# High-weight products of two blocks per unit at the head of a wide projection, and a later start of the modulation steps

## The reference, cut to what matters

```python
for l in range(DEPTH_2):
    mod = c_act @ w_ada[l] + b_ada[l]
    shift, scale, gate = jnp.split(mod, 3, axis=-1)
    h = _rmsnorm(x, norm_g[l]) * (1.0 + scale[:, None, :]) + shift[:, None, :]
    z = h @ w_in[l]                      # 2048 x 6656
    ...
    y = jnp.concatenate([o_fft, o_na, o_ret, o_cv], axis=-1) @ w_out[l]
    x = x + gate[:, None, :] * y
```

## Time and profile before

| | |
|---|---|
| median of the runs | 2070.2 us |
| the profiled execution | 2074.64 us |
| its span, first to last instruction | 2072.8 us |
| TensorE matmul, busy | 2032.5 us (98%) |
| TensorE weight load | 1642.6 us (79%) |
| VectorE | 1749.9 us (84%) |
| ScalarE | 1199.4 us (58%) |
| mean granted clock | 0.991 |
| mean transfer rate | 287 GB/s |

### The profile page before, as it was taken

How to read it: one execution, slowest core, us unless ns; L and a number is a source line. 1 busy time by engine, 2 the same in 40 slices (tenths; PEclk the granted TensorE clock), 3 DMA queues, 4 the chain that set the end, 5 groups by cost and what they waited for, 6 DMA issues and landing times.

```text
span 2072.8 us, 42606 instructions
## 1 busy us (share of the span) xinstructions
PE 2032.5 (98%) x18977; PEld 1642.6 (79%) x18977; DVE 1749.9 (84%) x1662; ACT 1199.4 (58%) x1079; POOL 58.3 (3%) x72
## 2 busy tenths in 40 slices
PE   8999999999999999999999999999999999999998
PEld 7889888888889946555555568888888888888887
DVE  7884798988888698999999989989967789899754
ACT  5553644444445488888877865465554444565543
POOL 0002300000000000000000000010000000100000
PEclk9999999999999999999999999999999999999999
DMA  7864487789898789999999977755857777558552
GB/s 282 323 221 145 163 316 284 275 315 328 321 329 300 282 310 405 420 420 420 420 420 418 411 274 263 258 192 201 291 199 287 271 290 255 196 203 293 181 203 102
DMA packets 96742, 595.27 MB, mean 287 GB/s; under 512 B 11176, under 2 KB 11336, under 8 KB 37808
## 3 DMA queue, kind: packets, MB, share of 16 engines
q1 hardware_dynamic: 94912, 583.66, 75.1%
q0 software_dynamic: 1648, 8.90, 1.1%
HBM read 588.32 MB, written 2.10 MB: 285 GB/s over the span
## 4 chain that ended last, share of the span: by engine, by line
PE 65%; issue 14%; DVE 11%; DMA 8%; ACT 2%; POOLq 0%; POOL 0%; DVEq 0%; ACTq 0%
PE GB L2274 43%; PE MB L2703 7%; PE GB L2703 6%; DVE w_lo L1321 3%; DMA W<-w_ada 3%; DMA Z<-w_ada 3%; DVE W L1321 2%; DMA raw<-w_down 2%; ACT w_hi L671 1%; DMA raw<-w_up 1%; DVE W L1292 1%; DVE Z L1292 1%; PE MB L2498 1%; PE MB L2474 1%; DVE Y L1382 1%
## 5 line engine op out<-in xcount | busy, mean ns | idle before, releaser
L1321 DVE SCALAR_TENSOR_TENSOR w_lo<-raw,w_hi 128x2048 f16<-128x2048 f32 x214 | 491.1, 2297 | 105.8 <-ACT w_hi L671 105.1
L671 ACT ACTIVATE w_hi<-raw 128x2048 f16<-128x2048 f32 x214 | 408.1, 1907 | 207.2 <-PE GB L2274 118.4
L2274 PE MATMUL GB<-H,w_hi 128*128 128x256 f16 x2880 | 476.0, 273 | 6.1 <-DVE w_lo L1321 4.3
L2274 PE MATMUL GB<-H,w_lo 128*128 128x256 f16 x1440 | 392.6, 273 | 0.0
L2274 PEld LDWEIGHTS GB<-H,w_hi 128*128 128x128 f16 x2880 | 279.5, 98 | 47.3 <-DVE w_lo L1321 6.4
L2274 PE MATMUL GB<-H,raw 128*128 128x256 f16 x2208 | 249.9, 273 | 8.3 <-DVE raw L1321 4.9
L2274 PEld LDWEIGHTS GB<-H,raw 128*128 128x128 f16 x2208 | 214.4, 98 | 40.1 <-DVE raw L1321 6.9
L1292 DVE SCALAR_TENSOR_TENSOR W<-W,SM 128x1024 f32<-128x1024 f32 x150 | 192.3, 1282 | 54.9 <-DMA W<-w_ada 51.4
L1321 DVE SCALAR_TENSOR_TENSOR raw<-raw 128x2048 f16<-128x2048 f32 x85 | 195.5, 2300 | 30.5 <-ACT raw L671 30.1
L671 ACT ACTIVATE raw<-raw 128x2048 f16<-128x2048 f32 x85 | 162.1, 1907 | 98.0 <-PE GB L2274 53.8
L2274 PEld LDWEIGHTS GB<-H,w_lo 128*128 128x128 f16 x1440 | 140.9, 98 | 16.4
(11 more groups left out here) (503 smaller groups left out, 3473.0 us busy)
## 6 DMA issues: line engine op xcount, KB each, us to landing
raw<-w_in SPq DMA_DIRECT2D x144, 1024.0 KB, 5.1
W<-w_ada SPq DMA_DIRECT2D x160, 512.0 KB, 5.8
raw<-w_out SPq DMA_DIRECT2D x48, 1024.0 KB, 5.9
raw<-w_down SPq DMA_DIRECT2D x35, 1024.0 KB, 13.3
raw<-w_up SPq DMA_DIRECT2D x29, 1024.0 KB, 12.5
raw<-w_gate SPq DMA_DIRECT2D x26, 1024.0 KB, 10.7
W<-w_down SPq DMA_DIRECT2D x17, 1024.0 KB, 13.1
raw<-xattn_wk SPq DMA_DIRECT2D x16, 1024.0 KB, 5.1
```

The costliest lines, as they stand in the source:

```text
L671: act.activation(w, raw_at[r], ACT.Copy, scale=W_SCALE).then_inc(hi_done, 1)
L1321: dve.scalar_tensor_tensor(lo, raw_at[r], W_SCALE, hi, ALU.mult, ALU.subtract).then_inc(raw_taken[r], 1)
L2274: last = pe.matmul(o, a, m, start=first, stop=end and w_part is lo, skip_group_check=True)
```

## The change

It has three parts. In `z0` and `z1` the first four blocks go through a new function `head` of TensorE: for each unit it takes the products with the high weights of two blocks (0 and 1, then 2 and 3), and after the last unit of the pair the products with their low weights, block by block, each block reported done after its low products. ScalarE makes the high splits of blocks 2 and 3 earlier, ahead of the units and after unit 6. The modulation steps of the two projections start with block 4 instead of block 2; of the 16, the three of blocks 2 and 3 are placed at 10, 11 and 13. `spread_root(3)` follows the four blocks.

```diff
     def halves(ph):
-        for m in [2, 2, 3, 4, 4, 5, 6, 6, 7, 8, 8, 9, 10, 12, 14, 16]:
+        for m in [4, 4, 5, 6, 6, 7, 8, 8, 9, 10, 10, 11, 12, 13, 14, 16]:
             put(ph, m)
...
             def shifted_hi(base, src, ph, shift):
+                split(ph, 2)
                 for n, unit in enumerate(UNITS):
                     act.wait_ge(S("norm_h"), base + n + 1)
...
                     if n == 6:
-                        split(ph, 2)
+                        split(ph, 3)
...
                 for m in range(4 * PIECES):
-                    if m >= 3:
+                    if m >= 4:
                         split(ph, m)
                     for i in nth(m, 3, 4, PIECES):
                         evict(i, 0)
...
+            def piece(ph, m, ks, parts, begins, ends):
+
+                s, (u, k) = where(ph, m)[1], (m % 2, m // 2)
+                ws = [a[slot(s)].rearrange("p (c n) -> p c n", c=8) for a in (hi_of, lo_of)]
+                for n in range(2):
+                    for c in ks:
+                        for x_low, w_low in parts:
+                            last = pe.matmul(GB[:, u, n * T:n * T + T], ws[w_low][:, c, n * P:n * P + P], (xh, xl)[x_low][:, 8 * k + c, :],
+                                             start=begins, stop=ends and c == ks[-1], skip_group_check=True)
+                            begins = False
+                return last
+
+            def head(ph, units, ready):
+
+                for k in range(2):
+                    for n, unit in enumerate(units):
+                        if unit[0] // 8 != k:
+                            continue
+                        first = unit[0] % 8 == 0
+                        pe.wait_ge(S("norm_lo"), ready + n + 1)
+                        for m in (2 * k, 2 * k + 1):
+                            s = where(ph, m)[1]
+                            if first:
+                                pe.wait_ge(hi_done, s + 1 + (s > at["z1"][1]))
+                                if k == 0:
+                                    pe.wait_ge(bank_free[m], uses[ph][m])
+                            piece(ph, m, [c % 8 for c in unit], ((0, 0), (1, 0)), first and k == 0, False)
+                    for m in (2 * k, 2 * k + 1):
+                        taken(pe, ph, m)
+                        piece(ph, m, range(8), ((0, 1),), False, k == 1).then_inc(block_done[where(ph, m)[1] % SPL], 1)
...
-                for m in range(4 * PIECES):
-                    if l == 0 and m == 3:
-                        spread_root(3, r_first)
+                head(ph, UNITS, 16 + 9 * l)
+                if l == 0:
+                    spread_root(3, r_first)
+                for m in range(4, 4 * PIECES):
```

## The result

The changed kernel took 2079.47 us (median of five, 2078.14 to 2085.42), the kernel before 2070.88 us beside it: a ratio of 1.0046, with a 95% interval of 1.0030 to 1.0061. The change makes the kernel slower by 8.6 us between the medians, 6 to 13 us by the interval; 2077.9 had been predicted, in a range of 2071.5 to 2082. The profiled execution was the slowest of the five, 2085.42 us with a span of 2083.5, so its sum has to be made against the 2074.6 of the profiled execution before: +10.8.

The account below looks back on a forecast made before the run. TensorE, busy for 98% of the span, was taken to bound the kernel. +4.2 us in `z0` and +3.5 in `z1` make +7.7 on the 2070.2 median: 2077.9 us, range 2071.5 to 2082.

Parts of the forecast that it names:

- Part 1, the head: First blocks of `z0` and `z1`: reordered products hide VectorE's chunk waits; -1.65 us up to block 3 in `z0`.
- Part 2, block 4: Unmoved eviction waits for block 2 and holds block 4: pauses 2.6 us (`z0`) and 3.2 (`z1`).
- rival (b): Block 4's splits are not held by the eviction, so the change is faster: -6.3 us, 2063.9; chance 0.06.
- Part 3, block 11: Modulation steps moved later delay VectorE's low split 11: block 11 +2.5 to +3.2 us (`z0`), +3.3 to +3.9 (`z1`).
- one more step is 1.2, or 1.9 with a wait of up to 0.7: VectorE between low splits 10 and 11: added modulation step costs 1.2 us, or 1.9 with a wait for its data.
- VectorE's idling between low splits 10 and 11 while TensorE pauses: Ahead of block 11: named as a sign that the prediction is wrong; no size given.
- The other queues: SP and GpSimd queues and `spread_root(3)` behind the head: zero, since final norms needing the spread stand behind low split 4.
- units 7 and 8: Chunk units late in the head: ready before TensorE asks, so nothing charged; the cover is 1.2 us.
- The clock: A half-clock stretch after block 4's pause costs 1.7 us of TensorE; counted zero, as block 11's pause swallows it.
- rival (c): Clock falls unswallowed, at block 11 or twice: +0.4 to +1.3 us per phase, up to 1.7 more; 2080.5; chance 0.14.
- The sum: Whole kernel: +4.2 us in `z0` and +3.5 in `z1`, together +7.7, giving 2077.9.

Follow-up runs that it names:

- changed, again: The changed kernel run once more with nothing edited (the sixth experiment), for a second profile: 2081.21 us, ratio 1.0040 to the kernel before.
- 1 evict behind: Changed kernel with ScalarE's eviction of piece 0, bank 0, put behind block 4's high split instead of ahead: 2069.68 us, ratio 0.9982.
- 2 steps back: Changed kernel with the modulation steps back at their old places, from block 2 on: 2075.36 us, ratio 1.0016.
- 3 steps only: Kernel before with only the modulation steps moved to block 4 on, its head unchanged: 2075.43 us, ratio 1.0008.
- 4 head only: 1 evict behind with the modulation steps at their old places: 2072.95 us, ratio 1.0001.
- 5 spread early: 1 evict behind with `spread_root(3)` also moved, ahead of block 2's low-weight products: 2066.26 us, ratio 0.9977.
- 7 no idle: Changed kernel with filler products of ones on TensorE, 22 (`z0`) or 28 (`z1`) ahead of block 4, 24 ahead of block 11: 2084.49 us, ratio 1.0061.
- 8 half the fillers: Changed kernel with 11 (`z0`) or 14 (`z1`) filler products ahead of block 4 and 11 ahead of block 11: 2080.00 us, ratio 1.0047.
- 9 first pair only: Changed kernel with only blocks 0 and 1 paired, blocks 2 and 3 in old order, three modulation steps at block 3: 2075.67 us, ratio 1.0021.
- 10 steps spread: 5 spread early with modulation steps starting at block 3, one instead of two at block 10, none at 11: 2068.55 us, ratio 0.9989.
- 11 small loads: Changed kernel with modulation loads of these stretches cut to a quarter of their bytes, read four times, steps unchanged: 2073.64 us, ratio 1.0012.

## Why the prediction was right

**Part 1, the head.** Forecast -1.65 us up to block 3 in `z0`. The table has the last group of blocks 3, 10 and 15, in us from the head's first product, read from TensorE's timelines.

```
kernel               z0: b3    b10    b15    z1: b3    b10    b15
before                24.10  61.39  88.63     23.70  61.19  87.69
changed               21.87  63.46  94.34     22.46  63.06  95.95
changed, again        21.87  61.79  91.79     21.87  63.19  91.72
1 evict behind        22.02  59.83  90.66     22.58  59.26  85.46
2 steps back          21.87  62.77  90.54     21.87  63.46  89.66
3 steps only          23.18  59.86  89.17     22.74  59.42  88.09
4 head only           21.87  63.06  90.83     22.60  61.35  88.48
5 spread early        22.30  58.98  88.58     21.87  58.55  85.16
7 no idle             21.87  63.89  95.45     21.87  64.80  96.36
8 half the fillers    21.87  61.79  91.40     21.87  61.79  90.44
9 first pair only     22.30  63.06  89.61     22.25  63.11  89.33
10 steps spread       22.30  62.02  89.02     21.87  59.02  85.22
11 small loads        21.87  63.26  89.55     22.57  62.49  88.68
```

Right: the head is 1.2 to 2.2 us shorter. In `z0` some 0.45 of that is the spread, which left block 3; with the spread counted in both kernels it is 1.8. The heads of 22.5 to 22.6 us in `z1` began with 3 us at 1.2 GHz (0.50 from 1658.50 to 1661.50 in the changed kernel); in the second execution that stretch was at 0.86, and the head took 21.87.

**Part 2, block 4.** The step that carried the prediction, and it held almost to the row. Forecast: eviction 20.35 us behind the head's start (1262.9 - 1242.55), measured 20.43 (1260.55 - 1240.12); low split 22.85, measured 22.86; block 4 25.15, measured 25.21; pauses 2.6 and 3.2, measured 2.63 + 0.16 and 3.07 + 0.16. The pause is decided by the order of two instructions in ScalarE's program: the one of experiment 1 took it away in both layers, the list of steps (experiment 2) and small loads (experiment 11) left it as it was. The whole loss hangs on it: the 1.0046 and 1.0040 become 0.9982 when the eviction alone is moved. What block 11 adds to it needs the late loads as well, since with small loads block 11 does not pause (experiment 11). With it fell rival (b): the split does not pass the eviction. The Trainium skill, "TensorE: Matmul & The Clock Gate", section "Architectural detail: the array is 16x 32x32, not 1x 128x128", says that ScalarE's and VectorE's queues are strictly first in, first out; the trace agrees: in this kernel and in those of experiments 2, 6 to 8 and 11 ScalarE idles 6.91 us, the eviction comes, and the split 0.49 to 0.50 us behind it.

**Part 3, block 11.** The mechanism was right, and the term for the load was too small. In the changed kernel low split 4 to 10 took 31.57 us in `z0` and 32.12 in `z1` (31.8 forecast). From 11 to 12 it took 1310.63 - 1304.35 = 6.28 and in `z1` 5.38; 6.29 and 5.38 had been forecast. What failed is 10 to 11: "one more step is 1.2, or 1.9 with a wait of up to 0.7", forecast 8.0 to 8.7 in `z0`, measured 9.80 (1304.35 - 1294.55) and 10.31 in `z1`. With small loads it is 8.20 (1294.26 to 1302.46), the working without the wait. So the step was sized nearly rightly (8.0 without a wait) and its load was not: 1.70 and 2.65 us of wait where 0.7 was the bound. The bound came from a wait at block 4, whose load had long been under way. The trace of before had longer ones in the same stretches, 1.16 us at 1294.72 in `z0`, and in `z1`:

```profile
1692.36 1.29 DVE L1292 SCALAR_TENSOR_TENSOR Z<-Z,SM 128x1024 f32<-128x1024 f32 x1 [2.38 <-DMA Z<-w_ada]
```

Low split 11 needs two steps, the second of which can load only when the step two before it has read its buffer; that chain should have been laid out. The prediction had named VectorE's idling between low splits 10 and 11 while TensorE pauses as a sign of being wrong. Half of it came: VectorE idled there, but 1.70 us that ended at 1300.51, while TensorE had products until 1303.57. Block 11 started 66.57 us behind the head in `z0` where it had been 62.53, +4.0 for a forecast of +2.5 to 3.2, and in `z1` 68.23 for 61.59, +6.6 for +3.3 to 3.9. In the second execution it was +1.5 and +3.6. For `z0` the forecast lies between the two executions, for `z1` at the lower one. That the total of 2077.9 came within 1.6 of the first median is for a part luck: the wait was put too small, and it varies by more than that from one execution to the next.

**The other queues.** Zero for `spread_root(3)` behind the head is right for the changed kernel and wrong as a price. VectorE had to wait for ScalarE until 1262.98 anyhow, and the spread was done at 1262.3. Experiment 1 took that cover off, and the spread cost VectorE 3.39 us. The prediction named no cover here, as it did for units 7 and 8.

**The clock.** Counted at zero, since the next pause, before block 11, was to swallow it. The clock fell behind block 4 of `z0`, and there it was swallowed as forecast: TensorE's last group of block 10 came at 63.46, 1.7 us later than at full clock, and VectorE let block 11 start only at 66.57. It also fell behind block 11, in both layers. Windows of the changed kernel from shortly behind block 4's start (the granted clock fell half a microsecond later) and from block 11 of `z0`, then from the same blocks of `z1`:

```profile
1265.87:1269.28 3.41, 3.41 (x18) 2.44 (x17) 3.31 (x4) 1.16 (x1) 0.00 (x0) 0.50 0.41 103
1306.69:1311.00 4.31, 4.31 (x25) 3.24 (x26) 4.27 (x9) 1.91 (x1) 0.00 (x0) 0.60 0.81 270
1684.30:1688.00 3.70, 3.70 (x34) 3.33 (x35) 3.59 (x3) 1.70 (x1) 0.00 (x0) 1.00 0.55 153
1726.66:1730.10 3.44, 3.38 (x16) 2.41 (x17) 3.44 (x8) 1.80 (x1) 0.00 (x0) 0.50 0.70 214
```

Nothing behind block 11 pauses long enough to give that back: blocks 11 to 15 took 27.7 to 27.8 us with such a stretch and 26.1 without one and without a pause (`z1` of experiment 1, both layers of experiment 9). That is rival (c)'s 1.7 us at block 11, in both layers of the first profile and one of the second. Where no late block 11 swallows it, the fall behind block 4 costs the same: from block 4's start to block 10's last group experiment 11 took 38.05 us in `z0`, with the fall, and 36.6 in `z1`, without, and experiment 9 took 38.25 in both layers, with it. Set against this, experiment 8 had no such stretch in its profile and no less time in its median, with the two reservations made there. So the step of counting the clock at zero holds at block 4 of `z0` alone; a fall costs 1.4 to 1.7 us where nothing swallows it, and how often one falls in the median execution stays open.

**The sum.** Forecast +4.2 and +3.5. The first profile has +5.7 and +8.3, nearly twice the forecast, the second (91.79 - 88.63, 91.72 - 87.69) +3.2 and +4.0, near it; the medians together +8.6 and +10.2. The mechanism at block 4 was right to a tenth of a microsecond; the load and the clock were both counted too small, and in the medians all that the forecast of +7.7 lacks is 0.9 and 2.5 us. What the runs do not explain: why the loads come so differently late in two executions of one kernel; and that the list of steps alone (+0.08%) and the rest alone (+0.16%) make +0.24%, against +0.40 to 0.46% for both, with intervals that allow the difference to be chance.

## What to carry to other kernels

When the producer of a result is moved later, look in every engine's program at who waits for that result, and at what stands behind the waiter. Here an eviction nobody touched turned a shorter head into a loss, and putting it behind the split that it blocked turned the loss into a gain of 0.2%. Work put off on an engine takes its loads along: price a step by the chain that frees its buffer and brings its data, and not by its own 1.2 us. And "hidden" always has a name: write down by which wait, since the fix of that wait is what uncovers it.

## What the runs showed of the hardware

- A float32 product of a 128x128 by a 128x128 operand of ones took TensorE 0.223 us at 2.4 GHz (22 of them from 1260.66 to 1265.57 in experiment 7), about as long as two of the fp16 products with 256 columns (0.109 each). Each product is shown as two records of 0.275 us, 0.112 apart. I had taken 0.107, and 0.21 for experiment 8.
- The granted clock did not follow from the length of a pause. It fell to 1.2 GHz behind pauses of 2.79 us (block 4 of `z0`), 3.01 and 5.06, and of 2.40 and 2.51 in experiment 9, and stayed at 2.4 GHz behind 3.23 us before block 4 of `z1` in the first execution (1.00 in the window at 1684.30); in the second execution of the same kernel the same 3.23 us pause was followed by 0.61 over 3.9 us, and the 2.79 of `z0` by 1.00 over the 3.5 us from block 4's start.
- The same block of 48 products took 5.42 us at full clock (1684.30 of the first execution) and 6.82 in the second, 1683.73, under that lower clock: 1.4 us for one fall.
